# Cache units of one batch with all eight heads, and the batches' softmax by halves, in a decoder step on one core

## What is computed

```python
s = jnp.einsum('bqhd,bqhnkd->bqhnk', qf, kg.astype(F32)) * scale
s = s - slopes[None, None, :, None, None] * dist.astype(F32)
s = jnp.where(ok[..., None] & (dist >= 0), s, -jnp.inf)
p = jax.nn.softmax(s.reshape(bt, q_block, nh, -1), axis=-1).reshape(s.shape)
out = jnp.einsum('bqhnk,bqhnkd->bqhd', p, vg.astype(F32))
```

## Time and profile before

| | |
|---|---|
| unprofiled runs | 1336.21, 1336.31 and 1333.51 us, median 1336.21 |
| profiled execution | 1332.85 us, its span from first to last instruction 1331.1 us |
| TensorE busy | 1273.9 us, 96% of the span |
| VectorE, ScalarE busy | 735.4 us (55%), 581.9 us (44%) |
| granted TensorE clock, mean | 0.984 |
| page transfers | 32 for keys and 32 for values, 256 KB each, median 3.0 and 3.4 us from issue to landing |
| transfers of w_ob | 4 of 1024 KB, median 8.1 us from issue to landing |

### The profile page before, as it was taken

The page is one execution under the profiler, slowest core; times in us unless marked ns, Lnnn a source line. Parts: engine busy times, 40 slices in busy tenths (PEclk is TensorE's granted clock), DMA queues, the critical chain, the costliest instruction groups (busy, mean ns, idle before and its releaser), DMA issues.

```text
span 1331.1 us, 22172 instructions
## 1 busy us (share of the span) xinstructions
PE 1273.9 (96%) x8841; PEld 1237.6 (93%) x8841; DVE 735.4 (55%) x1149; ACT 581.9 (44%) x922; POOL 102.7 (8%) x118
## 2 busy tenths in 40 slices
PE   6999999999999999999999999999995699999996
PEld 6999999998879999999999999999973599999996
DVE  7655645565666655655555655654544266566443
ACT  6444443443445554434435544533422255444332
POOL 2000001101423000000100000000300020000011
PEclk9999999999999999999999999999998799999998
DMA  8444345443233444334534544344548534433441
GB/s 294 154 158 149 106 142 169 165 143 109 84 115 128 158 158 157 117 122 152 202 136 169 203 158 141 113 134 149 190 147 272 216 127 159 157 134 121 132 151 39
DMA packets 40731, 200.54 MB, mean 151 GB/s; under 512 B 4938, under 2 KB 7114, under 8 KB 25178
## 3 DMA queue, kind: packets, MB, share of 16 engines
q1 hardware_dynamic: 38466, 192.37, 42.1%
q0 software_dynamic: 2208, 7.39, 1.7%
HBM read 193.17 MB, written 6.57 MB: 150 GB/s over the span
## 4 chain that ended last, share of the span: by engine, by line
PE 91%; SPq 2%; issue 2%; DVE 2%; DMA 1%; ACT 1%; POOL 0%; POOLq 0%; DVEq 0%; ACTq 0%
PE bank L407 29%; PE bank L409 29%; PE bank L408 28%; SPq L379 1%; SPq L380 1%; DMA raw<-vc_in 1%; PE bank L608 1%; PE bank L600 1%; DVE h_lo L1145 1%; PE bank L574 1%; DMA raw<-w_in 0%; PE bank L575 0%; PE bank L761 0%; DVE w_lo L1133 0%; PE bank L523 0%
## 5 line engine op out<-in xcount | busy, mean ns | idle before, releaser
L407 PE MATMUL bank<-h_hi,w_hi 128*128 128x320 f32 x1920 | 598.0, 311 | 16.4 <-DVE h_lo L1145 13.9
L409 PE MATMUL bank<-h_hi,w_lo 128*128 128x320 f32 x1920 | 594.7, 310 | 0.0
L408 PE MATMUL bank<-h_lo,w_hi 128*128 128x320 f32 x1920 | 594.6, 310 | 0.0
L825 ACT ACTIVATE w_hi<-raw 128x1024 fp32r<-128x1024 f32 (+1 forms) x368 | 336.0, 960 | 456.3 <-PE bank L409 451.6
L1133 DVE TENSOR_TENSOR w_lo<-raw,w_hi 128x1024 fp32r<-128x1024 f32 (+1 forms) x368 | 393.2, 1109 | 116.9 <-ACT w_hi L825 116.5
L407 PEld LDWEIGHTS bank<-h_hi,w_hi 128*128 128x128 f32 x1920 | 361.8, 188 | 20.6 <-DVE w_lo L1133 11.6
L408 PEld LDWEIGHTS bank<-h_lo,w_hi 128*128 128x128 f32 x1920 | 361.7, 188 | 0.2
L409 PEld LDWEIGHTS bank<-h_hi,w_lo 128*128 128x128 f32 x1920 | 361.6, 188 | 0.0
L408 PE MATMUL bank<-f_lo,w_hi 128*128 128x320 f32 x704 | 217.5, 309 | 0.0
L409 PE MATMUL bank<-f_hi,w_lo 128*128 128x320 f32 x704 | 217.4, 309 | 0.0
L407 PE MATMUL bank<-f_hi,w_hi 128*128 128x320 f32 x704 | 217.4, 309 | 0.0
(11 more groups left out here) (190 smaller groups left out, 666.1 us busy)
## 6 DMA issues: line engine op xcount, KB each, us to landing
raw<-w_in SPq DMA_DIRECT2D x88, 1024.0 KB, 4.8
raw<-w_out SPq DMA_DIRECT2D x64, 704.0 KB, 4.1
raw<-w_a SPq DMA_DIRECT2D x12, 1024.0 KB, 4.8
raw<-w_kv SPq DMA_DIRECT2D x8, 1024.0 KB, 4.7
raw<-kc_in SPq DMA_DIRECT2D x32, 256.0 KB, 3.0
raw<-vc_in SPq DMA_DIRECT2D x32, 256.0 KB, 3.4
raw<-w_oa SPq DMA_DIRECT2D x4, 1024.0 KB, 5.5
raw<-w_q SPq DMA_DIRECT2D x4, 1024.0 KB, 4.8
```

The source lines that it names most:

```text
L407: pe.matmul(out, wh, mh, start=first, stop=False)
L408: pe.matmul(out, wh, ml, start=False, stop=False)
L409: return pe.matmul(out, wl, mh, start=False, stop=last)
L825: sc.activation(w_hi[:, n_at % 2, part * w:part * w + w], raw[:, raw_of(n_at) % RAW, part * w:part * w + w], ACT.Copy).then_inc(hi_done, 1)
```

## The change

A cache unit now holds one batch with all eight heads: two transfers of whole pages (128 rows of 4 KB, 512 KB) take the place of four of 256 KB. Key unit b gives scores to two banks, those of both groups of heads in b's half of the batches. So the banks are finished in pairs: banks 0 and 2 (batches 0 to 3) after key unit 3, banks 1 and 3 after unit 7. Softmax of the batches is done in these pairs, in the order 0, 2, 1, 3, at heads 2 and 4 of the prompt. TensorE's order is rewritten: cache unit 0 comes ahead of the loop, and each head has units 2h + 1 and 2h + 2. ScalarE and VectorE split w_ob 0 and w_ob 1 both at head 6. At the end the outputs of batches 4 to 7 are copied, turned and split in two parts, one copy by ScalarE and one by VectorE (`last_rows`), and the output projection waits for its input tile by tile. The order of loads on the sync engine is the same.

```diff
-                for j in range(2 * NPG):
-                    at = 2 * NPG * (c % 4) + j
+                for j in range(NPG):
+                    at = NPG * (c % NB) + j
                     page = sp.value_load(pages[0:1, at:at + 1], min_val=0, max_val=kc_in.shape[0] - 1)
-                    sp.dma_start(raw[:, r % RAW, j * 512:j * 512 + 512],
-                                 src[bass.ds(page, 1), :, heads].rearrange("a p c -> p (a c)")
+                    sp.dma_start(raw[:, r % RAW, j * 1024:j * 1024 + 1024],
+                                 src[bass.ds(page, 1), :, :].rearrange("a p c -> p (a c)")
                                  ).then_inc(loaded[r % RAW], 16)
...
+            def cache_scores(b):
+                raw_at = raw_of_cache(b)
                 pe.wait_ge(loaded[raw_at % RAW], loads_after(raw_at))
...
+                for h in range(H):
+                    k, out = h % QB, bank[2 * (h // QB) + b // 4]
+                    mm = pe.matmul(out[SLOT * k:SLOT * k + SLOT, 0:PAST], q_spread[:, h, b // 4, own],
+                                   keys[:, :, h, :], start=False, stop=(b % 4 == 3), skip_group_check=True)
                 mm.then_inc(kv_used, 1)
...
+            def cache_outputs(b):
+                raw_at, q = raw_of_cache(NB + b), b // 4
+                outs = [bank[4][:, DV * g:DV * g + DV] if q == 0 else bank[2 * g][:, 0:DV] for g in range(2)]
...
+                if b % 4 == 0:
+                    pe.wait_ge(sm_tc, 6 * q + 6)
...
+                    if g == 0 and b == NB - 1:
+                        mm.then_inc(sm_og, 1)
                 mm.then_inc(kv_used, 1)
...
+            def turn_early_outputs():
+                pe.wait_ge(sm_oc, 2)
+                for g in range(2):
+                    mm = pe.transpose(bank[4][:, g * 128:g * 128 + 128], o_rows[:, 2 * g, :], ident)
                 mm.then_inc(sm_ot, 1)
+            def turn_late_outputs(g):
+                if g == 0:
+                    pe.wait_ge(pr_b, H)
+                    pe.wait_ge(sm_oc, 3)
+                else:
+                    pe.wait_ge(sm_lo, 1)
+                    pe.wait_ge(sm_od, 1)
+                pe.transpose(bank[5 - g][:, 0:128], o_rows[:, 2 * g + 1, :], ident).then_inc(sm_ot, 1)
...
+            cache_unit(0)
             for h in range(H):
...
+                cache_unit(2 * h + 1)
                 prompt_turn(h)
                 if h + 1 < H:
                     prompt_scores(h + 1)
...
+                    if h in (2, 4):
+                        turn_probs(h - 2)
+                    cache_unit(2 * h + 2)
+                    prompt_outputs(h)
+                    if h in (2, 4):
+                        turn_probs(h - 1)
+                    if h == 6:
+                        turn_early_outputs()
+            turn_late_outputs(0)
+            turn_late_outputs(1)
+            prompt_outputs(H - 1)
             def attended_at_kt(kt):
...
-            pe.wait_ge(pr_lo, H)
+                pe.wait_ge(pr_lo, kt + 1)
+                pe.wait_ge(sm_lo, kt // 4 + 2)
```

On ScalarE:

```diff
                 prompt_exp(h)
-                if 1 <= h <= 4:
+                if h in (2, 4):
+                    sample_exp(h - 2)
                     sample_exp(h - 1)
+                if h == 6:
+                    split_at(U_OB)
+                    sc.wait_ge(kv_used, NB + 4)
+                    sc.wait_ge(sm_r, 2)
+                    sample_rows(0, bank[4][:, 0:DV])
+                    sample_rows(2, bank[4][:, DV:2 * DV])
                 if h >= 1:
                     prompt_hi(h - 1)
                 if h == 6:
-                    sample_rows(0)
-                    split_at(U_OB)
-            sample_hi(0)
-            split_at(U_OB + 1)
+                    split_at(U_OB + 1)
+            early_hi()
+            sc.wait_ge(sm_og, 1)
+            sc.wait_ge(sm_r, 3)
+            sample_rows(1, bank[0][:, 0:DV])
             prompt_copy(H - 1)
+            late_hi(0)
+            late_hi(1)
             prompt_hi(H - 1)
-            sample_rows(1)
-            sample_hi(1)
```

On VectorE:

```diff
                 prompt_bias(h)
-                if 1 <= h <= 4:
+                if h in (2, 4):
+                    sample_bias(h - 2)
                     sample_bias(h - 1)
+                if h in (3, 5):
+                    spread_probs(h - 3)
+                if h == 6:
+                    split_at(U_OB)
                 prompt_probs(h)
                 if h >= 1:
                     prompt_lo(h - 1)
-                if 2 <= h <= 5:
+                if h in (3, 5):
                     spread_probs(h - 2)
                 if h == 6:
-                    split_at(U_OB)
-            sample_lo(0)
-            split_at(U_OB + 1)
+                    split_at(U_OB + 1)
+            early_lo()
+            last_rows()
+            late_lo(0)
+            late_lo(1)
             prompt_lo(H - 1)
-            sample_lo(1)
```

More of the change, by code:

```diff
@@ L255, in trunk_program @@
         sm_tc = sem("sample_probs_spread")
+        sm_og = sem("sample_first_heads_finished")
         sm_oc = sem("sample_outputs_copied")
+        sm_od = sem("sample_outputs_copied_by_vector")
         sm_ot = sem("sample_outputs_transposed")
@@ L275, in trunk_program @@
         CACHE = 2 * NB
+        ORDER = (0, 2, 1, 3)
         P_A = FK
@@ L301, in loads_after @@
         def loads_after(r):
-            return sum(16 if cached_at(q) is None else 64 for q in range(r % RAW, r + 1, RAW))
+            return sum(16 if cached_at(q) is None else 16 * NPG for q in range(r % RAW, r + 1, RAW))
         def raw_of(n):
@@ L719, in new_scores, with turn_probs @@
                               k_all[:, h, t:t + SLOT], start=True, stop=False, skip_group_check=True)
-            def cache_scores(c):
-                raw_at, g, j = raw_of_cache(c), c // 4, c % 4
-                r = 2 * g + j // 2
+            def cache_scores(b):
+                raw_at = raw_of_cache(b)
                 pe.wait_ge(loaded[raw_at % RAW], loads_after(raw_at))
[L726 to L732, removed]
+                keys = raw[:, raw_at % RAW, :].rearrange("p (g h k) -> p g h k", g=NPG, h=H)
+                own = slice(SLOT * (b % 4), SLOT * (b % 4) + SLOT)
+                for h in range(H):
+                    k, out = h % QB, bank[2 * (h // QB) + b // 4]
+                    mm = pe.matmul(out[SLOT * k:SLOT * k + SLOT, 0:PAST], q_spread[:, h, b // 4, own],
+                                   keys[:, :, h, :], start=False, stop=(b % 4 == 3), skip_group_check=True)
                 mm.then_inc(kv_used, 1)
-            def turn_probs(r):
-                pe.wait_ge(sm_e, r + 1)
+            def turn_probs(i):
+                r = ORDER[i]
+                pe.wait_ge(sm_e, i + 1)
                 for pg in range(NPG):
@@ L741, in turn_probs @@
                 pe.transpose(bank[r][0:w, 256:384], ss[:, r, PAST + SLOT - w:PAST + SLOT], ident).then_inc(sm_t, 1)
[L743 to L753, removed]
+            def cache_outputs(b):
+                raw_at, q = raw_of_cache(NB + b), b // 4
+                outs = [bank[4][:, DV * g:DV * g + DV] if q == 0 else bank[2 * g][:, 0:DV] for g in range(2)]
+                own = slice(SLOT * (b % 4), SLOT * (b % 4) + SLOT)
+                if b % 4 == 0:
+                    pe.wait_ge(sm_tc, 6 * q + 6)
+                    for h in range(H):
+                        k, r = h % QB, 2 * (h // QB) + q
+                        pe.matmul(outs[h // QB][SLOT * k:SLOT * k + SLOT, :],
+                                  p_new[:, r, SLOT * k:SLOT * k + SLOT], v_tok[:, 2, h, 0:DV],
+                                  start=(b > 0 or h < QB), stop=False, skip_group_check=True)
@@ L754, in cache_outputs @@
                 pe.wait_ge(loaded[raw_at % RAW], loads_after(raw_at))
-                for s in range(2):
-                    b = 2 * j + s
-                    own = slice(SLOT * (b % 4), SLOT * (b % 4) + SLOT)
+                for g in range(2):
+                    r = 2 * g + q
                     for pg in range(NPG):
                         for k in range(QB):
[L760 to L763, removed]
+                            v = pg * 1024 + (QB * g + k) * 128
+                            mm = pe.matmul(outs[g][SLOT * k:SLOT * k + SLOT, :],
+                                           p_spread[:, pg, r, k, own], raw[:, raw_at % RAW, v:v + 128],
+                                           start=False, stop=(b % 4 == 3 and pg == 1), skip_group_check=True)
+                    if g == 0 and b == NB - 1:
+                        mm.then_inc(sm_og, 1)
@@ L778, in _, with cache_unit @@
             pe.wait_ge(qa_sp, 2)
+            def cache_unit(c):
+                if c < NB:
+                    cache_scores(c)
+                else:
+                    cache_outputs(c - NB)
+            cache_unit(0)
             for h in range(H):
[L780 to L783, removed]
+                cache_unit(2 * h + 1)
                 prompt_turn(h)
```

(17 more changed lines are left out.)

48 lines of the change are left out of this document (21 added, 27 removed).

## The result

The changed kernel took 1314.15 us in the median of four runs (1311.76 to 1315.12), the kernel before beside it 1334.86 (1332.68 to 1336.31): ratio 0.9844, 95% interval 0.9822 to 0.9865. That is 20.7 us less; the forecast was 1313.0 in a range of 1306 to 1322. The profiled execution took 1313.96 us with a span of 1312.2.

What follows compares the result with a forecast made beforehand. The sync engine's page issue was taken to bound the attention stage; 989.2 + 10x (unit 12), 10.5 + x (to unit 15) and 5.0 put the output projection at 1034.0, 21.9 us earlier: 1313 us, range 1306 to 1322.

Steps and rivals of the forecast that it cites:

- What bounds the kernel: Attention stage: TensorE waits 27.5 us for pages; the sync engine's 1.10 us per 256 KB issue, 4.4 us per unit, limits.
- The transfers, x = 2.66: Page loads: a 1 MB unit costs the DMA engines x = 2.66 us (394 GB/s); unit 12 lands at 1015.8.
- The pace: TensorE, attention heads: 4.31 us per head, +1.0 us each at heads 2 and 4; turn 5 at 1009.8.
- units 5 to 11 waited for: Sign in the attention stage: TensorE waiting for these units would show the step on transfers wrong, x over 2.8.
- The path to the end: End of attention: unit 12 to unit 15's landing 13.1 us, then 5.0 us; output projection starts at 1034.0.
- The new waits: End of attention: sm_og and sm_od beside turn 7 and its copy cost 0, at most 0.7 us.
- The sum: Start of output projection = 1004.7 + 11x = 1034.0 instead of 1055.86: 21.9 us less.
- Two of the signs of being wrong: Attention stage: w_ob 0 landing after 1013 would show the end wrong; turn 5 starting after 1012, the pace wrong.
- A: Rival, DMA engines: they keep the time of small rows, x = 3.3; gain 14.9 us, 1318 to 1321; chance 0.11.
- B: Rival, page loads: fetching pages, not the sync engine, sets 4.4 us per unit; gain 2.8 us, about 1332; chance 0.04.
- C: Rival, slower: pages at the first window's 202 GB/s, 5.2 us per unit; start 6 us later, about 1340; chance 0.03.
- D: Rival, transfers: rows still cut to 2 KB, x between 2.66 and 3.3; counted in the forecast's 0.82.

Runs made afterwards that it cites:

- e2: Kernel before with the 16 page numbers read into registers once ahead of the first cache load, transfers and order unchanged: 1320.09 us, ratio 0.9894.
- e1: Changed kernel with each 512 KB page transfer cut into two of 256 KB, a register load ahead of each: 1327.45 us, ratio to before 0.9955.
- e3: Changed kernel with 256 KB transfers (2 KB rows) and page numbers read into registers ahead: 1315.39 us, ratio to before 0.9857.
- e4: Changed kernel with w_ob 1 split at head 6 ahead of prompt_hi(5) on ScalarE and prompt_lo(5) on VectorE: 1308.68 us, ratio to before 0.9813.
- e11: Kernel before with page numbers in registers and w_ob 1 split at head 6 directly behind w_ob 0: 1307.92 us, ratio 0.9803.
- e5: Changed kernel with all 16 cache units loaded ahead of w_ob 0 to 3, both splits behind the last unit: 1305.26 us, ratio to before 0.9786.
- e6: Changed kernel with page numbers read into registers ahead: 1311.67 us, ratio to before 0.9828.
- e8: The changed kernel itself, run again on the same chip as three others: 1312.50 us, ratio to before 0.9839.
- e12: Changed kernel with all cache units ahead of all weights and both splits behind the last unit, run again: 1305.14 us, ratio to before 0.9779.
- e9: Changed kernel with all pages first, but w_ob 0 loaded between units 14 and 15 and split beside unit 15: 1304.45 us, ratio to before 0.9776.
- e10: The kernel of e9 with page numbers read into registers ahead: 1303.03 us, ratio to before 0.9761.

## Why the prediction was right

**What bounds the kernel.** Right. That the sync engine paced the pages is shown by e2, which makes issue cheap and nothing else, by e1, which makes it dear again, and by e3, which takes the register loads away from e1 and gets 12.1 us back. The row behind it was the 1.10 us between two issues beside DMA engines that were 75% busy. Of the Trainium skill, "DMA: Bandwidth & Descriptors", section "Issuing engines are not separate DMA queues" says that the time to initiate a DMA is usually small relative to it; for 256 KB with a register load ahead, 1.10 us against 0.66, this case's runs don't agree, though the issue instruction alone is 0.33. The Trainium skill, same page, section "Where 436 GB/s comes from" has loads from HBM bound near 358 GB/s for a core, which it works out as half of what a stack gives to two cores; on the one core that this kernel uses, the changed kernel's pages came at 415.

**The transfers, x = 2.66.** The size was a little high: 1.049 MB at 415 GB/s is 2.53 us once the queue is full. But unit 4 landed 5.5 us after the release, not 4.8, for its two transfers go out 1.09 us apart and the second takes 4.38 us by itself. Units 5 and 6 took 3.6 and 3.5 us each, as the windows with 211 and 281 GB/s show. Unit 12 landed 33.1 us after the first issue (1019.03 less 985.92), forecast 31.4: +1.7, of which the first three units are +2.5 and the eight after them -0.8.

**The pace.** Turn 5 came 25.5 us after turn 0, forecast 24.3. The steps at heads 2 and 4 with two bias-and-maximum steps ahead of prompt_probs were 5.0 and 5.3 us (5.3 forecast). The claim that no unit before 12 is waited for was wrong: units 5, 6, 7, 9 and 11 cost 0.7, 0.8, 0.3, 0.8 and 0.3 us, from the slow first units. It cost nothing at the end, since unit 12 was late anyway. By the prediction's own sign, units 5 to 11 waited for, the step on transfers was wrong; what was wrong in it is the landing of the first three units, not the x over 2.8 that the sign was meant to show.

**The path to the end.** From unit 12 to unit 15: 13.96 us, forecast 13.15. The step that failed in size is the landing of unit 15: I priced it as a lone 1 MB transfer, 4.96 us. Its two transfers go out 1.09 us apart and the second takes 4.88 us by itself, together 5.97. After unit 15: 4.1 us, forecast 5.0, since the granted clock was back at 1.00 from 1036 on and the projection follows prompt_outputs(7) without a gap. TensorE's last wait was 5.24 us, not 2.3, and the first of the three 4.78, not 4.4. e4 shows that the tie of unit 15 to unit 12 is real and worth 4 to 5.5 us.

**The new waits.** sm_og and sm_od cost nothing visible: the late turns (0.58 us) are over before the copy of turn 7 is.

**The sum.** Errors of +1.7, +0.8 and -0.9 us leave the start 1.6 us late (51.14 for 49.58). The step priced too high takes back about a third of what the two priced too low had cost, which is luck. The forecast of 21.9 us less became 20.3 in the stage, 20.7 in the medians. That the forecast of 1313 lies 1.2 us from the measured median owes something to the choice of the base between 1332.85 and 1336.21; the gain is the better test, and it was 1.2 to 1.6 us too large. Two of the signs of being wrong were set by the clock of the old execution, a first landing of w_ob 0 after 1013 and a turn 5 after 1012; they came at 1013.95 and 1012.51, but the stage began 1.5 us later here, and counted from the first released transfer both are inside (28.0 and 26.6 us, against 28.6 and 27.6).

**The rivals.** A falls with e3, B and C with e2: with cheap issues the pages come at 395 GB/s even in half-page transfers. D did not occur: the page counts 36121 DMA packets instead of 40731, and 16 MB in rows of 4 KB instead of 2 KB are 4096 fewer.

What I did not see is that the larger part of the edit was not needed (e11), and that the two weight loads between the pages were the dearest thing left (e5).

## What to carry to other kernels

Where waits for loads stand beside DMA engines at 75%, measure the issuing engine's own period: here the register load with its address steps made up more than half of the 1.10 us from one transfer to the next, and reading the numbers once was worth 13.7 us, where the whole change gave 20.7. Once the queue is full, the order in it and what releases its slots decide: find the last load that waits for a slot, and move what holds the slot (a split of a weight unit standing behind an unrelated copy) before touching the size of anything. A forecast for such a stage can be made as one sum along the queue and one along the chain from the late load to the end; price a load issued in parts as the parts' spacing plus the last one's landing.

## What the runs showed of the hardware

Of pages that were queued up after a pause, the first moved slowly in the changed kernel: 211 GB/s from 986 to 990 us and 281 from 992 to 994, then 414 and more, though issues ran ahead from the start. Part of the 211 is the time to the first landing (the first of these 4 us moved data at 37 GB/s), but the next three ran at 262 to 274. Unit 6 landed 12.6 us after the first release there and 11.7 to 12.2 us in e4, e5, e6, e8 and e12; the 5.97 us that unit 15 took alone and two units at full rate would make 11.0. Why was not tried. In e9 and e10 TensorE waited nearly the same time for unit 15, 2.92 and 2.95 us, but only in e10 did the granted clock fall (windows, first of e9, then of e10), so here a wait of that length did not by itself fix at which of the two levels the next matmuls run:

```profile
1024.00:1028.00 4.00, 3.81 (x50) 3.18 (x47) 2.06 (x5) 2.23 (x6) 0.00 (x0) 1.00 1.00 397
```

```profile
1024.00:1028.00 4.00, 3.62 (x39) 2.76 (x40) 1.75 (x4) 1.20 (x4) 0.00 (x0) 0.62 1.01 420
```
